# Two norms around a residual: the second sum of squares taken from three sums made beside the products, and products begun on several outputs at once

## The chip, the cores and the metric

One core of one Trainium2 chip. The metric is the time of one launch in microseconds (us). Weights and inputs lie in the chip's DRAM in float32. The names of the engines are those of the profile: PE is TensorE (matmuls), PEld its weight loads, DVE VectorE, ACT ScalarE, POOL GpSimd, SP the queue that issues nearly all weight loads.

## The reference, cut to what matters

The program is two blocks of a network, one behind the other, on 256 tokens ("latents") of width 1024, the second block with 256 context tokens beside them. The change lies in the second block, where each of two layers does this (`fn` is the mixer first, and a gated convolution FFN then):

```python
def rmsnorm(x, g):
    xf = x.astype(jnp.float32)
    y = xf * lax.rsqrt(jnp.mean(xf * xf, axis=-1, keepdims=True) + EPS)
    return (y * g.astype(jnp.float32)).astype(x.dtype)

hl = modulate(rmsnorm(xl, norm_g[layer, 0]), mod_l[0], mod_l[1])
...
xl = xl + mod_l[2] * rmsnorm(yl, norm_g[layer, 1])
hl = modulate(rmsnorm(xl, norm_g[layer, 2]), mod_l[3], mod_l[4])
xl = xl + mod_l[5] * rmsnorm(conv_ffn(hl, ...), norm_g[layer, 3])
```

So between two big products stand two norms in a row: the output y of the one is normed and added to the residual x, and the new x is normed again, scaled and shifted, to be the input h of the next. With r the inverse root of y's mean square and Y = gate·g·y, the new x is X + r·Y, and its sum of squares is sum(X·X) + 2r·sum(X·Y) + r²·sum(Y·Y). Layer 0 does this for context and latents (512 columns), layer 1's mixer for both and the rest for the latents alone (256 columns).

## The kernel before, in words

Activations lie transposed in SBUF: 8 tiles (KD = 8) of 128 features each by 512 columns of tokens, 256 of context (CTX) and 256 of latents (LAT). `k.X` is the residual, `k.H` the input of a product, `Y` the gated output of one. Weights stream through a ring of 11 slots of 1 MB ("units" of 16 tiles of 128 by 128, RING = 11, UT = 16); SP refills a slot when the last matmul of its unit is done (`refill`). A product with 8 input tiles is `gemm` (L255): output after output, and within one the 8 input tiles. Its results go to PSUM banks 0 to 3 in turn. A matmul of the program is two records on PE in the trace.

Each stage is an `nc.Block()`: every engine has its own list there, and the next block starts when all have ended theirs. The change touches three crossings from one block to the next, called here:

- **A**, layer 0: from `stage_square` (the mixer's output product, 512 columns) to `stage_conv_ffn` (the FFN's up products, 512 columns);
- **B**, from layer 0's FFN (its down product) to `stage_rwkv_project`, layer 1's first products, whose input is shifted and mixed on DVE (XX, XB) tile by tile, and whose first 8 outputs are for the 256 latents;
- **C**, layer 1: from `stage_square` to `stage_conv_ffn`, 256 columns each.

At each the class `AfterY` (L629) does the work. While the product before runs, `Beside` has ACT square each output (L579) and POOL add up outputs 0 to 6 (L586). Behind the last output, in the next block: PE sums those squares over features with matmuls against a column of ones (`add_up`, L508, one for each 128 columns), DVE, ACT and DVE take mean, root and inverse (L516, L523, L518), PE spreads the inverse over all partitions of bank 5 (`to_all`, L528), and DVE scales Y by it (`part`, L654). DVE adds the even tiles of Y to X (L657), POOL the odd ones (L664). ACT squares each tile of the new X (L673) into one of two buffers, PE adds it up (L508, 32 matmuls at 512 columns), ACT waits for PE to give a buffer back. Then mean, root, inverse and spread once more, and DVE scales X into H (L613), ACT scales and shifts H for each half (L621), and the product waits for its input tiles one by one (L272, `ready`). At B the DVE makes, behind all of that, -h (L3026), two shifted additions (L3016) and the mixed input (L3020) of each tile.

The modulation of the next layer is itself a product, of 24 units, run beside layer 0's FFN (`Modulation.unit`, L306: four matmuls of 32 rows by 512 columns); `weave` sets where its units stand among the FFN's in the order of weights, in pairs after every few units. `Finish` copies, turns and takes its result during the FFN's last outputs.

The edit also touches `Plan`, `woven` (the order of the weights in DRAM) and `block2_even` and its like for layer 1, where the objects are made.

## Time and profile before

| | |
|---|---|
| median of 3 runs | 3330.53 us (3325.06 to 3331.04) |
| the profiled execution | 3328.68 us, span 3326.8 us, mean granted clock of TensorE 0.952 |
| PE busy | 3102.2 us, 93% of the span |
| DVE busy | 1033.2 us, 31% |
| ACT busy | 587.9 us, 18% |
| POOL busy | 230.6 us, 7% |
| DMA | 577.07 MB, 173 GB/s over the span |

In the rows further down, a row of the timeline gives start and duration in us, engine, line, operation, output<-input, the count of instructions merged, and in brackets how long the engine sat idle before and what ended that. A row of the windows gives the window, and for each engine the busy us and (x) instructions, then the granted clock of TensorE (1.00 is 2.4 GHz, 0.50 is 1.2 GHz) and the share and rate of DMA. Matmul ends are modelled.

### The profile page before, as it was taken

Reading aid. Unit: us, or ns where it says so; the run is one execution under the profiler, and the core shown is the slowest. Engines: PE = TensorE matmul, PEld = TensorE weight load, DVE = VectorE, ACT = ScalarE, POOL = GpSimd, SP = SyncE. Lnnn points to the kernel's source line nnn. Section 1 sums busy time; section 2 is a strip of 40 time slices with the busy share of each in tenths; the row PEclk is TensorE's granted clock in tenths of the full one; section 3 lists DMA queues with packets and bytes.
Section 4 is the critical chain, followed back from the end, with each engine's and each line's share of the span. In section 5 each row is a group of like instructions: output and inputs, shape, how many; then the busy total and the mean of one; then the engine's idle time right before and its main releaser. Section 6 shows DMA issues by size and latency. Waiting matters only on the chain. (4 is left out here: it accounts for less than half of the span.)

```text
span 3326.8 us, 54854 instructions
## 1 busy us (share of the span) xinstructions
PE 3102.2 (93%) x24374; PEld 1905.5 (57%) x24374; DVE 1033.2 (31%) x2267; ACT 587.9 (18%) x1333; POOL 230.6 (7%) x205
## 2 busy tenths in 40 slices
PE   7999998999999999899888999999897888888998
PEld 5899884533333333446664444444645687777887
DVE  4365105211101110240451433400404555651650
ACT  1011113200000000220342100000203434432100
POOL 0000000000000000000221000000001231220000
PEclk8999999899999999899898999999798999897999
DMA  9755549499988899520003133333111000004340
GB/s 378 301 187 218 181 171 421 165 383 391 390 347 361 359 386 398 240 76 26 3 1 139 76 127 139 127 126 126 57 38 48 25 15 14 14 3 191 128 151 13
DMA packets 88494, 577.07 MB, mean 173 GB/s; under 512 B 9536, under 2 KB 15936, under 8 KB 20672
## 3 DMA queue, kind: packets, MB, share of 16 engines
q1 hardware_dynamic: 84800, 568.27, 43.8%
q10 hardware_dynamic: 3456, 5.24, 0.4%
q8 instruction: 195, 3.19, 0.4%
q14 instruction: 43, 0.35, 0.0%
HBM read 567.19 MB, written 6.29 MB: 172 GB/s over the span
## 5 line engine op out<-in xcount | busy, mean ns | idle before, releaser
L272 PE MATMUL ps<-H,ring 128*128 128x256 f32 (+1 forms) x2480 | 805.0, 487 | 12.3 <-ACT H L621 7.0
L272 PEld LDWEIGHTS ps<-H,ring 128*128 128x128 f32 x2480 | 478.2, 194 | 335.5 <-issue 298.1
L272 PE MATMUL ps<-W,ring 128*128 128x256 f32 (+1 forms) x1616 | 497.1, 469 | 13.4 <-DVE W L3020 8.0
L1865 PE MATMUL ps<-ring,W 128*32 128x512 f32 (+1 forms) x2816 | 461.4, 594 | 1.7 <-ACT H L1924 1.7
L272 PEld LDWEIGHTS ps<-W,ring 128*128 128x128 f32 x1616 | 309.3, 193 | 200.8 <-issue 170.5
L1865 PEld LDWEIGHTS ps<-ring,W 128*32 128x32 f32 (+1 forms) x2816 | 142.5, 123 | 306.7 <-issue 304.1
L1888 PE MATMUL ps<-ring,W 128*64 128x512 f32 (+1 forms) x1408 | 231.1, 594 | 0.0
L2146 DVE SCALAR_TENSOR_TENSOR W<-ps,vec,W 128x189 f32<-128x189 f32 (+3 forms) x396 | 173.3, 438 | 14.0
L3545 POOL TENSOR_TENSOR ring<-ring 128x512 f32<-128x512 f32 x96 | 124.5, 1313 | 526.2 <-DVE ring L3569 458.8
L1888 PEld LDWEIGHTS ps<-ring,W 128*64 128x64 f32 (+1 forms) x1408 | 70.9, 123 | 156.9 <-issue 156.9
L306 PE MATMUL ps<-ring,spread 128*32 128x512 f32 x768 | 101.1, 634 | 23.3 <-DMA ring<-weights 18.8
L1973 DVE TENSOR_TENSOR H<-ps,H 128x256 f32<-128x256 f32 x66 | 28.0, 425 | 303.5 <-ACT H L1915 303.5
L1915 ACT ACTIVATE H<-ps 128x256 f32<-128x256 f32 x66 | 25.3, 383 | 459.8 <-PE ps L1865 459.8
L2132 DVE TENSOR_SCALAR W<-ps,vec 128x512 f32<-128x512 f32 (+1 forms) x44 | 29.8, 677 | 235.1 <-PE ps L272 235.1
L3421 PE MATMUL ps<-ring 64*64 64x64 f32 x2560 | 89.9, 220 | 13.7 <-DVE ring L3659 13.6
L2168 ACT ACTIVATE W<-W 128x512 f32<-128x512 f32 (+1 forms) x44 | 23.0, 523 | 440.8 <-DVE W L2146 440.8
L3421 PEld LDWEIGHTS ps<-ring 64*64 64x64 f32 x2560 | 82.3, 134 | 18.8 <-issue 18.7
L3654 DVE TENSOR_TENSOR W<-W,ps 128x512 f32<-128x512 f32 x80 | 53.8, 672 | 120.2 <-PE ps L3436 120.2
L1020 PE MATMUL ps<-W 128*128 128x128 f32 x744 | 88.3, 275 | 0.0
L1020 PEld LDWEIGHTS ps<-W 128*128 128x128 f32 x744 | 85.5, 192 | 0.0
L3436 PE MATMUL ps<-W,ring 64*64 64x64 f32 x2560 | 83.7, 218 | 0.4 <-issue 0.4
L3436 PEld LDWEIGHTS ps<-W,ring 64*64 64x64 f32 x2560 | 79.7, 134 | 0.6 <-issue 0.5
(447 smaller groups left out, 3138.6 us busy)
## 6 DMA issues: line engine op xcount, KB each, us to landing
ring<-weights SPq DMA_DIRECT2D x528, 1024.0 KB, 7.9
rkv<-W ACTq DMA_DIRECT2D x16, 256.0 KB, 2.0
ring<-rkv SPq DMA_DIRECT2D x8, 512.0 KB, 3.6
X<-tokens SPq DMA_DIRECT2D x2, 1024.0 KB, 8.9
ring<-rw_tiles SPq DMA_DIRECT2D x8, 256.0 KB, 2.6
rkv<-W ACTq DMA_DIRECT2D x8, 128.0 KB, 2.3
ring<-rkv SPq DMA_DIRECT2D x8, 128.0 KB, 3.7
out<-X SPq DMA_DIRECT2D x8, 128.0 KB, 1.9
```

Of the source, the lines that this page charges most:

```text
L272: mm = pe.matmul(out(o), lhsT=k.ring[:, k.slot(at), p * P:(p + 1) * P], rhs=rhs(kk), start=kk == 0 and not (shared_bank and o % 2), stop=k ...
L306: mm = pe.matmul(k.ps[32 * q:32 * q + 32, self.bank, :], lhsT=self.spread[:, 4 * half + q, start:start + 32], rhs=k.ring[:, k.slot(place), ...
L1020: mm = pe.matmul(self.bank(bank), lhsT=a[:, kk * P:(kk + 1) * P], rhs=b[:, kk, :], start=start and kk == 0, stop=stop and kk == 3, skip_gr ...
L1865: mm = pe.matmul(ps[at:at + n, r, :], lhsT=moe.Hg[:, kt, FIRST * e + first:FIRST * e + first + n], rhs=w[e][:, kk * WIDE:(kk + 1) * WIDE], ...
L1888: mm = pe.matmul(ps[to:to + n, 3 - 3 * half + r, :], lhsT=moe.A[:, f, r, to:to + n], rhs=w[e][:, at:at + 512], start=f == 0, stop=f == KF - 1,
L1973: dve.tensor_tensor(moe.G[:, r, :], ps[:, r, S:2 * S], moe.G[:, r, :], ALU.mult).then_inc(sem["g"].sem, 1)
L2132: link(dve.tensor_scalar(y, x, w(1, 1), k.v("fcb", layer * KF + f), ALU.mult, ALU.add))
L2146: ins = dve.scalar_tensor_tensor(yo, xo, ww, yo, ALU.mult, ALU.add)
L3421: mm = pe.matmul(ps[half(e), bank, CH * n:CH * n + CH], lhsT=sc.OT[z][l % 2][half(e), n, :], rhs=sc.M[z][half(e), n, :], start=True, stop= ...
L3436: mm = pe.matmul(ps[half(e), bank, CH * n:CH * n + CH], lhsT=sc.T1[z][half(e), n, :], rhs=sc.MT[j % 2][z][half(e), n, :], start=True, stop ...
L3545: pool.tensor_tensor(sc.OT[z][l % 2], lt, sc.level[z][l].unsqueeze(1).to_broadcast([P, 8, CH]), ALU.mult).then_inc(sem["ot"], 1)
L3654: add = dve.tensor_tensor(flat(MT), flat(MT), ps[:, (4 + 4 * (l - 1) + z) % 3, :], ALU.add)
```

## The change

1. `Ahead` takes the place of `Beside` at A, B and C. While the product before runs, DVE multiplies each output Y with X and with itself and adds these up over outputs 0 to 6 (`cross`). PE sums the three running totals (squares, X·Y, Y·Y) right behind its last matmul, still in the old block (`add_totals`), and in the new block only what belongs to the last output (`add_last`). The kept sum of X·X (`sums_of_x`) is brought up to date on DVE from the three sums, with four small operations, and its root and inverse are spread to bank 7. The 8 squares of the new X on ACT and their sums on PE are gone.
2. `AfterY.vector` works tile by tile: part, change, scale (tiles 0 and 1), then in pairs, with POOL adding tiles 3, 5 and 7.
3. The FFN's up products begin with outputs 0 and 1 abreast, input tile by input tile; in layer 0 the first 8 modulation units stand among them, one ahead of each input tile (`early`).
4. In `stage_rwkv_project` the first 8 outputs run abreast, two to a PSUM bank of 512 columns, for each input tile as it comes. DVE shifts and mixes a tile right behind scaling the next one (`then`), and -h is made by ACT. The copies out of PSUM start when both outputs of a bank are done; the next outputs wait for the copies of theirs.

```diff
-def weave(units, more):
+def weave(units, more, early=0):
-    order, v = [], 0
+    order, v = [(1, i) for i in range(early)], early
...
+class Ahead(Beside):
+    SUMS = 7
...
+    def cross(self, dve, link, o, Y):
+        y = Y[:, o, 0:self.n]
+        at = 2 if o == 0 else o % 2
+        for t, x in ((self.xy, self.k.X[:, o, self.cols]), (self.yy, y)):
+            ins = dve.tensor_tensor(t[at], x, y, ALU.mult)
...
+        if 1 <= o < KD - 1:
+            link.wait()
+            for t in (self.xy, self.yy):
+                ins = dve.tensor_tensor(t[2], t[2], t[at], ALU.add)
...
+    def add_totals(self, pe):
+        pe.wait_ge(self.added.sem, self.added.at(KD - 2))
+        self.add_up(pe, self.total, self.blocks)
+        pe.wait_ge(self.crossed.sem, self.crossed.at(2))
+        self.cross_up(pe, self.xy[2], 0)
+        self.cross_up(pe, self.yy[2], NB)
+
+    def add_last(self, pe):
+        pe.wait_ge(self.squares.sem, self.squares.at(KD))
+        self.add_up(pe, self.sq[1], self.blocks).then_inc(self.sums.sem, 1)
+        pe.wait_ge(self.crossed.sem, self.crossed.at(3))
+        self.cross_up(pe, self.xy[1], 0)
+        pe.wait_ge(self.crossed.sem, self.crossed.at(4))
+        self.cross_up(pe, self.yy[1], NB).then_inc(self.cross_sums.sem, 1)
...
 class AfterY(Norm):
+    PARTS, BY_POOL, OWN = (0, 1, 3, 2, 5, 4, 7, 6), (3, 5, 7), (0, 1, 2, 4, 6)
...
     def tensor(self, pe):
-        self.before.add_tiles(pe)
+        self.before.add_last(pe)
         self.before.to_all(pe)
-        for i in range(KD):
-            pe.wait_ge(self.rms.squares.sem, self.rms.squares.at(i + 1))
-            mm = self.rms.add_up(pe, self.sq[i % 2], self.rms.blocks)
-            mm.then_inc(self.rms.sums.sem if i == KD - 1 else self.summed.sem, 1)
         self.rms.to_all(pe)
...
+    def vector(self, dve, then=lambda i: None, later=0):
...
+        before.cross(dve, link, KD - 1, Y)
+        dve.wait_ge(before.sums.sem, before.sums.at(1))
...
+        dve.wait_ge(before.cross_sums.sem, before.cross_sums.at(1))
...
+        link(dve.tensor_tensor(tail, both[:, 1, own], r, ALU.mult))
+        link(dve.scalar_tensor_tensor(tail, both[:, 0, own], 2.0, tail, ALU.mult, ALU.add))
+        link(dve.tensor_tensor(tail, tail, r, ALU.mult))
+        link(dve.tensor_tensor(x, x, tail, ALU.add))
+        dve.tensor_scalar(rms.r[:, own], x, 1.0 / D, EPS, ALU.mult, ALU.add).then_inc(rms.mean.sem, 1)
...
+        for i in (0, 1):
+            part(i)
+            change(i)
+            if i == 0:
+                dve.wait_ge(rms.spread.sem, rms.spread.at(1))
+            scaled(i)
+        for i in (2, 4, 6):
+            part(i + 1)
+            part(i)
+            change(i)
+            scaled(i)
+            scaled(i + 1)
...
@@ stage_square @@
             gemm(k, pe, 8, KD, lambda kk: k.H[:, kk, cols], lambda o: k.ps[:, o % 4, 0:n], before, signals)
+            rms.add_totals(pe)
...
+            for o in range(KD - 1):
+                dve.wait_ge(k.act.sem, k.act.at(o + 1))
+                rms.cross(dve, link, o, Y)
...
@@ stage_conv_ffn @@
-    p = Plan(owner, ada.units)
+    p = Plan(owner, ada.units, early=min(KD, ada.units))
...
-                 plan=p, ada=ada, ready=pre.ready)
+                 plan=p, ada=ada, ready=pre.ready, abreast=2,
+                 more=(lambda kk: ada.unit(pe, p.place[1, kk], kk)) if ada.units else None)
...
+            for o in range(KD - 1 if ahead else 0):
+                dve.wait_ge(k.act.sem, k.act.at(KF + o + 1))
+                rms.cross(dve, link, o, Y)
...
@@ stage_rwkv_project @@
+    place = lambda o: k.ps[:, o // 2, (o % 2) * S:(o % 2) * S + S]
...
-                    if first_o + o >= 4:
-                        pe.wait_ge(k.act.sem, k.act.at(first_o + o - 3))
+                        pe.wait_ge(k.act.sem, k.act.at(2 * o + 2 if n == 1 and o < 4 else first_o + o - 3))
+                if n == 0:
+                    gemm(k, pe, KD, KD, lambda kk: XB[0][:, kk, LAT], place, before, signals, abreast=KD, shared_bank=True,
+                         ready=lambda eng, kk: eng.wait_ge(k.dve.sem, k.dve.at(kk + 1)))
+                    continue
...
+            def then(j):
+                if j >= 1:
+                    shift(j - 1)
+                    dve.wait_ge(shifted.sem, shifted.at(2 * j))
+                    mixed(0, j - 1)
+
+            pre.vector(dve, then, later=1)
```

The last FFN (layer 1) still ends with `Beside`, and `stage_last` is as before.

PE at crossing A, from the last product of `stage_square` into the FFN, before (a branch ends a block; L508 are the sums against ones, L528 the spreads):

```order
L272 MATMUL ps<-H,ring 128x512 x64
L2043 UNCONDITIONAL_BRANCH
L2101 UNCONDITIONAL_BRANCH
L508 MATMUL ps<-const,W 128x1 x8
L528 MATMUL ps<-const,sm 128x128 x4
L508 MATMUL ps<-const,W 128x1 x32
L528 MATMUL ps<-const,sm 128x128 x4
L272 MATMUL ps<-H,ring 128x512 x48
L306 MATMUL ps<-ring,spread 32x512 x8
```

and in the changed kernel (L632 are the sums of X·Y and Y·Y):

```order
L272 MATMUL ps<-H,ring 128x512 x64
L508 MATMUL ps<-const,W 128x1 x4
L632 MATMUL ps<-const,W 128x1 x8
L2140 UNCONDITIONAL_BRANCH
L2204 UNCONDITIONAL_BRANCH
L508 MATMUL ps<-const,W 128x1 x4
L632 MATMUL ps<-const,W 128x1 x8
L528 MATMUL ps<-const,sm 128x128 x8
L306 MATMUL ps<-ring,spread 32x512 x4
L272 MATMUL ps<-H,ring 128x512 x2
L306 MATMUL ps<-ring,spread 32x512 x4
L272 MATMUL ps<-H,ring 128x512 x2
```

Twelve sums stand ahead of the end of the block and twelve behind it, the 32 are gone, and a modulation unit (4 of L306) stands ahead of each pair of product matmuls.

DVE at crossing B, before, from the second mean to the first mixed tile (L613 scales X, L3026 is -h, L3016 the shifted additions, L3020 the mixing):

```order
L516 TENSOR_SCALAR sm<-ps 128x4
L518 RECIPROCAL sm<-sm 128x4
L613 TENSOR_TENSOR H<-X,ps 128x512 x8
L3026 TENSOR_SCALAR W<-H 128x512 x2
L3016 TENSOR_TENSOR W<-W,H 128x255
L3016 TENSOR_TENSOR W<-W,H 128x4x63
L3026 TENSOR_SCALAR W<-H 128x512
L3016 TENSOR_TENSOR W<-W,H 128x255
L3016 TENSOR_TENSOR W<-W,H 128x4x63
L3020 SCALAR_TENSOR_TENSOR W<-W,vec,H 128x256
```

and now (L726 part, L730 change, L737 scale, L3129 shifted additions, L3133 mixing):

```order
L726 TENSOR_TENSOR W<-W,ps 128x512
L730 TENSOR_TENSOR X<-X,W 128x512
L737 TENSOR_TENSOR H<-X,ps 128x512
L726 TENSOR_TENSOR W<-W,ps 128x512
L730 TENSOR_TENSOR X<-X,W 128x512
L737 TENSOR_TENSOR H<-X,ps 128x512
L3129 TENSOR_TENSOR W<-W,H 128x255
L3129 TENSOR_TENSOR W<-W,H 128x4x63
L3133 SCALAR_TENSOR_TENSOR W<-W,vec,H 128x256
L726 TENSOR_TENSOR W<-W,ps 128x512 x2
L730 TENSOR_TENSOR X<-X,W 128x512
L737 TENSOR_TENSOR H<-X,ps 128x512
```

The first mixed tile stands behind 6 full-width operations of DVE and its own 3, where 8 scalings, with the parts and changes of all tiles ahead of them, stood before it.

## Rows read from the trace of the kernel before

**Rows 1.** The page: busy time, share of the span, instructions.

```profile
PE 3102.2 (93%) x24374; PEld 1905.5 (57%) x24374; DVE 1033.2 (31%) x2267; ACT 587.9 (18%) x1333; POOL 230.6 (7%) x205
```

**Rows 2.** Timeline of crossing A, from the last product to the first.

```profile
1789.63 22.05 PE L272 MATMUL ps<-H,ring 128*128 128x512 f32 x51
...
1812.22 0.83 ACT L780 ACTIVATE W<-ps,sm 128x256 f32<-128x256 f32 x2
...
1813.35 2.14 PE L508 MATMUL ps<-const,W 128*128 128x1 f32 x16 [1.67 <-PEq L2043]
1815.54 0.16 DVE L516 TENSOR_SCALAR sm<-ps 128x4 f32<-128x4 f32 x1 [58.85 <-PE ps L508]
...
1816.20 2.07 PE L528 MATMUL ps<-const,sm 128*128 128x128 f32 x8 [0.70 <-DVE sm L518]
1818.31 1.28 DVE L654 TENSOR_TENSOR W<-W,ps 128x512 f32<-128x512 f32 x2 [2.17 <-PE ps L528]
1819.51 0.69 DVE L657 TENSOR_TENSOR X<-X,W 128x512 f32<-128x512 f32 x1
1819.67 7.04 POOL L664 TENSOR_TENSOR X<-X,W 128x512 f32<-128x512 f32 x4 [12.88 <-DVE W L654]
...
1820.92 13.81 PE L508 MATMUL ps<-const,W 128*128 128x1 f32 x64 [2.64 <-ACT W L673]
...
1837.54 4.87 DVE L613 TENSOR_TENSOR H<-X,ps 128x512 f32<-128x512 f32 x8 [2.16 <-PE ps L528]
1838.27 7.97 ACT L621 ACTIVATE H<-H,mod 128x256 f32<-128x256 f32 x16 [3.10 <-DVE H L613]
```

**Rows 3.** Timeline of PE alone behind crossing A.

```profile
1839.51 44.47 PE L272 MATMUL ps<-H,ring 128*128 128x512 f32 x96 [2.00 <-ACT H L621]
1883.91 1.92 PE L306 MATMUL ps<-ring,spread 128*32 128x512 f32 x16
```

**Rows 4.** Windows at crossing A: the clock is the figure before the DMA share.

```profile
1814.00:1817.00 3.00, 2.30 (x16) 2.21 (x15) 0.34 (x2) 0.20 (x1) 0.00 (x0) 0.65 0.62 259
...
1845.00:1848.00 3.00, 3.00 (x7) 1.24 (x7) 0.00 (x0) 2.52 (x4) 0.00 (x0) 0.90 0.00 0
```

**Rows 5.** Timeline of crossing B and of ACT's copy of the eighth output.

```profile
2303.48 19.13 PE L272 MATMUL ps<-W,ring 128*128 128x512 f32 x44
...
2353.70 0.74 DVE L3016 TENSOR_TENSOR W<-W,H 128x255 f32<-128x255 f32 x2
...
2355.37 0.48 DVE L3020 SCALAR_TENSOR_TENSOR W<-W,vec,H 128x256 f32<-128x256 f32 x1
...
2355.99 2.53 PE L272 MATMUL ps<-W,ring 128*128 128x256 f32 x4 [7.79 <-DVE W L3020]
...
2391.07 0.38 ACT L3050 ACTIVATE W<-ps 128x256 f32<-128x256 f32 x1 [3.07 <-PE ps L272]
```

**Rows 6.** A window at crossing B, where the clock rises.

```profile
2365.00:2369.00 4.00, 4.00 (x13) 3.24 (x13) 4.00 (x7) 0.38 (x1) 0.00 (x0) 0.64 0.10 33
```

**Rows 7.** Timeline of crossing C, and a window where the clock rises.

```profile
3049.65 15.70 PE L272 MATMUL ps<-H,ring 128*128 128x256 f32 x72
...
3078.68 1.22 PE L528 MATMUL ps<-const,sm 128*128 128x128 f32 x4 [0.69 <-DVE sm L518]
3079.94 2.74 DVE L613 TENSOR_TENSOR H<-X,ps 128x256 f32<-128x256 f32 x8 [1.31 <-PE ps L528]
...
3081.14 17.08 PE L272 MATMUL ps<-H,ring 128*128 128x256 f32 x70 [1.24 <-ACT H L621]
...
3084.00:3086.00 2.00, 2.00 (x10) 1.68 (x9) 0.00 (x0) 1.71 (x2) 0.00 (x0) 0.84 0.00 0
```

**Rows 8.** Four outputs abreast in layer 0's first product: timeline and window.

```profile
1396.58 30.33 PE L272 MATMUL ps<-H,ring 128*128 128x512 f32 x64 [1.27 <-ACT H L746]
...
1401.00:1404.00 3.00, 3.00 (x7) 1.30 (x6) 2.81 (x10) 2.32 (x5) 0.00 (x0) 0.85 0.00 0
```

**Rows 9.** Weight loads early in layer 0's FFN: count, KB, median us to landing.

```profile
ring<-weights SPq DMA_DIRECT2D x6, 1024.0 KB, 4.8
```

More of the change, by code:

```diff
@@ L198, with __init__ @@
 class Plan:
-    def __init__(self, owner, more=0, seven=0):
+    def __init__(self, owner, more=0, seven=0, early=0):
         self.product = {}
         self.units = -(-len(owner) // UT)
-        self.order = weave(self.units, more)
+        self.order = weave(self.units, more, early)
         self.place = {x: i for i, x in enumerate(self.order)}
@@ L629, with __init__ @@
 class AfterY(Norm):
-    def __init__(self, k, cols, scale, shift, before, sq, Y):
-        super().__init__(k, cols, scale, shift, Rms(k, "after", range(cols.start // P, cols.stop // P), 404))
+    PARTS, BY_POOL, OWN = (0, 1, 3, 2, 5, 4, 7, 6), (3, 5, 7), (0, 1, 2, 4, 6)
+    def __init__(self, k, cols, scale, shift, before, Y):
+        super().__init__(k, cols, scale, shift, Rms(k, "after", range(cols.start // P, cols.stop // P), 404, squares=0))
+        self.rms.SPREAD = 7
         self.before, self.Y, self.n = before, Y, cols.stop - cols.start
-        self.sq = [x[:, 0:self.n] for x in sq]
-        self.part, self.changed, self.summed = k.shared("part", KD), k.shared("changed", KD // 2), k.shared("summed", KD - 1)
-        self.odd = k.shared("odd_changed", KD // 2)
+        self.part, self.changed, self.odd = k.shared("part", KD), k.shared("changed", KD - 3), k.shared("odd_changed", 3)
+        self.sums_of_x, self.tail = k.sm[:, 408:412], k.sm[:, 412:416]
@@ L660, in pool, with scalar @@
     def pool(self, pool):
         k, cols = self.k, self.cols
-        for i in range(1, KD, 2):
-            pool.wait_ge(self.part.sem, self.part.at(i + 1))
+        for i in self.BY_POOL:
+            pool.wait_ge(self.part.sem, self.part.at(self.PARTS.index(i) + 1))
             pool.tensor_tensor(k.X[:, i, cols], k.X[:, i, cols], self.Y[:, i, 0:self.n], ALU.add).then_inc(self.odd.sem, 1)
-    def scalar(self, act):
+    def scalar(self, act, then=lambda i: None):
+        k = self.k
         self.before.take_root(act)
+        self.rms.take_root(act)
@@ L668, in scalar @@
         for i in range(KD):
-            done = self.odd if i % 2 else self.changed
-            act.wait_ge(done.sem, done.at(i // 2 + 1))
-            if i >= 2:
-                act.wait_ge(self.summed.sem, self.summed.at(i - 1))
-            act.activation(self.sq[i % 2], self.k.X[:, i, self.cols], ACT.Square).then_inc(self.rms.squares.sem, 1)
-        super().scalar(act)
+            act.wait_ge(self.normed.sem, self.normed.at(i + 1))
+            for h, c in self.halves:
+                ins = act.activation(k.H[:, i, c], k.H[:, i, c], ACT.Identity, scale=self.scale(i, h), bias=self.shift(i, h))
@@ L678 @@
+            ins.then_inc(self.h.sem, 1)
+            then(i)
 class AfterFirst(Norm):
@@ L2071, in stage_square, with stage_conv_ffn @@
     k.unit += U_SQ
-def stage_conv_ffn(k, layer, cols, Y, ada, pre, rms, finish=None):
+def stage_conv_ffn(k, layer, cols, Y, ada, pre, rms, finish=None, ahead=True):
     nc = k.nc
@@ L2119, in _ @@
                  signals, first=down0 * KD, plan=p, ada=ada)
+            if ahead:
+                rms.add_totals(pe)
         @block.vector
@@ L3043, in _, with then @@
         def _(act):
-            pre.scalar(act)
+            def then(i):
+                pre.ready(act, i)
+                act.activation(XX[:, i, :], k.H[:, i, :], ACT.Copy, scale=-1.0).then_inc(turned.sem, 1)
+            pre.scalar(act, then)
             for o in range(24):
-                act.wait_ge(k.mm.sem, k.mm.at(out_done[o]))
+                act.wait_ge(k.mm.sem, k.mm.at(out_done[o | 1 if o < KD else o]))
                 if o >= 4:
@@ L3049, in _ @@
                 c = tokens(o // 8)
-                act.activation(out[:, o % 4, c], k.ps[:, o % 4, c], ACT.Copy).then_inc(k.act.sem, 1)
+                act.activation(out[:, o % 4, c], place(o) if o < KD else k.ps[:, o % 4, c], ACT.Copy).then_inc(k.act.sem, 1)
                 act.wait_ge(k.act.sem, k.act.at(o + 1))
@@ L3738, in wide_units, with woven @@
     return w.reshape(2, 4, P, n // WIDE, WIDE).transpose(3, 0, 2, 1, 4).reshape(-1, P, 4 * WIDE)
-def woven(own, *more):
+def woven(own, *more, early=0):
     more = np.concatenate(more)
-    return np.stack([more[u] if kind else own[u] for kind, u in weave(len(own), len(more))])
+    return np.stack([more[u] if kind else own[u] for kind, u in weave(len(own), len(more), early)])
 def cols(v):
```

96 lines of the change are left out of this document (66 added, 30 removed).

## The prediction, made blind

> **What bounds the kernel now.** I read the page first: PE is busy 93% of the span, the other engines a third or less [rows 1]. So time can come only out of stretches in which PE has nothing useful to do or does it at half clock. The change touches three crossings (A, B, C), and the timeline of each shows such a stretch. At A the last product ends at 1811.68 (1789.63 + 22.05) and the next starts at 1839.51 [rows 2, 3]: 27.8 us. At B it is 2322.61 to 2355.99, 33.4 us [rows 5], and at C 3065.35 to 3081.14, 15.8 us [rows 7]. PE is not idle all that time: at A 64 records of sums take 13.81 us [rows 2], which is the second sum of squares. The windows give the clock: at A the mean of 0.65 over 1814 to 1817 means that it fell at about 1814.9, 3.2 us behind the last product and in spite of the sums that ran, and 0.90 over 1845 to 1848 that it rose at about 1845.6, 6.1 us behind the first product [rows 4]. At B it rose at 2367.9, 11.9 us behind the first, thinly spaced products [rows 6], at C at 3084.6, 3.5 us behind [rows 7].
>
> Behind each crossing PE runs without a gap (96 records in 44.47 us at A, 70 in 17.08 at C [rows 3, 7]), so I take it that what a crossing gives goes to the end of the program. The sum is made against the profiled execution, 3328.7 us; the median of the runs is 1.8 above it. A measurement of this kernel tells some 0.2%, 6.7 us, from no change.
>
> **Prices.** A product record of 512 columns takes 22.05 / 51 = 0.432 us [rows 2], one of 256 columns 15.70 / 72 = 0.218 [rows 7]. A sum record takes 2.14 / 16 = 0.134 with the clock mostly full and 13.81 / 64 = 0.216 at half. A spread takes 2.07 [rows 2], at C 1.22 [rows 7]. A block ends 0.30 us behind its last engine (ACT ends at 1813.05, PE starts at 1813.35), and three small steps on DVE, ACT, DVE take 1816.20 - 1815.54 = 0.66, 0.22 each [rows 2].
>
> **Crossing A.** The sums of the totals are 12 matmuls, 24 records, right behind the last product: 3.2 us, to 1814.9; they replace ACT's tail to 1813.05 as what ends the block, and 0.3 more gives 1815.2. `add_last` is 24 records. All at half clock, as the clock falls just there: 5.2, to 1820.4 (3.2 if it fell later; that is the bound below). DVE's two multiplications of the last output (0.69 each, by the addition L657 [rows 2]) and its mean and inverse lie beside that. Then the two spreads, 4.1, to 1824.5: the second needs the new chain on DVE, four small operations and the three steps, 0.88 + 0.66 = 1.5 us behind the last sum, less than the first spread takes. Part and change of tile 0 (1.4) also fit beside the second spread. From scaling to product took 1839.51 - 1837.54 = 1.97 [rows 2, 3]: the first product would start at 1826.5, 13.0 earlier. But a modulation unit (1.92 / 2 = 0.96 us [rows 3], twice that at half clock) now stands ahead of it, needs nothing of the norm and fills those 2 us. So PE's useful work begins at 1824.5 where it began at 1839.5: **15.0 us**. The loss to half clock behind it was 44.47 - 96 x 0.432 = 3.0 us and I keep it.
>
> Do the tiles come fast enough? DVE makes 8 parts, 5 changes and 8 scalings at 0.6 to 0.69, 1.9 us a tile; PE wants 4 records and a unit a tile, 2.7 at full clock. POOL's addition takes 7.04 / 4 = 1.76 beside DVE [rows 2], and DVE comes back to it behind a part, a change and a scaling, 1.9: just in time. So PE never waits behind tile 0. The early units also want weights sooner: the first refill is asked for at the first unit and lands in 4.8 us [rows 9], and 11 slots are full at the start, where a unit of products lasts 13.8 us. I cost that at nothing; if the loads took 13.8 each, each would show whole.
>
> **Crossing B.** Same steps: 2322.61 + 3.2 + 0.3 + 5.2 + 4.1 = 2335.4. Then DVE scales tile 0, makes part, change and scaling of tile 1 (2.7), two shifted additions (0.74), the mix (0.48) and two short waits: 4.1, to 2339.5, 16.5 earlier than 2355.99 [rows 5]. The eight outputs took from there to 2391.07, 35.1 us; their 128 records want 27.9, and the rest was half clock and DVE's pace. Abreast, each tile is 3.5 us of work on arrival, so PE has no gap and I charge only 3.0 for the clock, as at A: 30.9, to 2370.4. **20.7 us.** DVE's pace is 5.9 us for two tiles (five operations of 0.69 at most, two times 1.27), the last tile is mixed at 2358.3, and PE needs it at 2366.9. The copies out of PSUM, now bunched, stand behind each other at 0.38 and an issue: ACT has bank 0 free about when PE wants it. The -h on ACT (0.6 a tile) lies beside DVE.
>
> **Crossing C.** 12 records of totals 1.6, 0.3, 12 of `add_last` 2.6: 3069.85. Here the DVE chain (1.5) is longer than the spread (1.22): 3071.35, spread to 3072.6, scaling to product 3081.14 - 3079.94 = 1.2 [rows 7]: 3073.8, 7.3 earlier. The clock took 1.8 before (17.08 - 70 x 0.218); it may take 3.0 now. I take **6.7 us**. DVE's pace is 0.98 a tile against 0.87 for two outputs abreast, but PE starts at half clock and behind.
>
> **The products beside** pay nothing: DVE's four operations for an output, under 2.8 us, fit into the 6.9 us of one at A (3.5 and 1.7 at C), where DVE is idle. Behind output 6 come ACT's tail (1811.68 to 1813.05 at A) and these four, so its totals are ready 6.9 - 1.4 - 2.8 = 2.7 us before PE asks, at C about 3.5 - 0.8 - 1.7 = 1.0.
>
> Sum: 15.0 + 20.7 + 6.7 = 42.4. From 3328.7 that is 3286.3, from the median 3288.1; I say 3287.
>
> **A rule against it.** The program already runs four outputs abreast, in four banks in turn: 64 records in 30.33 us, and 0.85 over 1401 to 1404 puts the rise of the clock at 1401.9, 5.3 us behind the start [rows 8]. So cycling banks did not keep the clock low there, with 512 columns and no other matmuls between. The Trainium skill, "TensorE: Matmul & The Clock Gate", section "A second HAM failure mode: psum-queue depth-cycling", says that a product which cycles through PSUM banks leaves PE idle for short moments and the clock swings between its levels. By that rule the abreast parts would lose most of what they give; the row speaks against it, but no row has units of 32 rows between, nor eight outputs of 256 columns two to a bank.
>
> **The rivals.**
> - *The clock stays low longer.* At B it took 11.9 us to rise behind thin work [rows 6]. If that is the measure everywhere, each crossing loses 6.0 instead of 3.0, 3.0 and 2.4: 9.6 us, 3297. For it: sums and 32-row units may count for little, as the sums did at 1814.9. Against it: A and rows 8, both dense, 5.3 and 6.1. Chance 0.12.
> - *DVE becomes the bound at B.* If waits between its steps make a tile 4.5 us, the last is mixed at 2371.0 and the outputs end at 2374.5, 4.1 later: 3291. It decides from 4.1 us a tile on. Against it: the pace above comes from rows with the same waits. Chance 0.06.
> - *Slower: the clock does not rise at all while outputs run abreast.* The place is the first tiles behind each crossing. Their work is 8 x (1.73 + 0.96) = 21.5 at A, 27.9 at B, 7.0 at C, in all 56.4 us at full clock; at half it costs 56.4 more, then 3.0 on each plain run behind, less the 8.4 already in the sum: 57.0 against 42.4. That is 14.6 slower than the median before, 3345. It decides once more than about three quarters of that work runs at half. Against it [rows 8]. Chance 0.03.
> - *The change doesn't do what it says*: the totals wait in PE's queue for DVE, or the small chain takes the place of the squares. Even then the squares of X are gone, with 13.8 us of sums at A [rows 2] and as much at B; some 2 us at each crossing come back, 3293. Chance 0.04.
>
> **How the numbers follow.** The forecast has the remaining 0.75. Its own bounds: `add_last` at full clock gives 4 us more, a rise of the clock after 3.5 us another 2.6, the lowest of the runs 5: 3275. Above, the low clock and a little of a DVE pace: 3299. So 3275 to 3299. Faster by more than 6.7 us in all cases but the slower one and oddities: 0.95; within 0.2%: 0.02; slower 0.03.
>
> **What would show it.** In the changed profile: 24 short records right behind the last product and 24 behind the branch; no squares of X on ACT; first product about 15 us (modulation unit), 16.5 and 7.3 us earlier relative to the last product; at B the eighth output's copy some 48 us behind the last product instead of 68; the clock at 1.00 within 6 us of the first dense work. Wrong would be: PE idle between tiles, a clock of 0.50 through the abreast part, or PE waiting for DMA behind the early units.

## The result, and the profile after

The changed kernel takes 3272.97 us (median of 4 runs, 3269.43 to 3274.41) against 3329.82 for the kernel before beside it. The ratio is 0.983, 95% interval 0.9813 to 0.9847: **56.9 us faster**. The forecast was 42.4 us, 3287, with a range down to 3275, so the sign was right, the forecast gain was too small, and the time fell below the range. The profiled execution took 3269.43 us, a span of 3267.5 against 3326.8, 59.3 less, at a mean granted clock of 0.962 against 0.952.

The page of the changed kernel, which answers to [rows 1]: PE has 80 records fewer and is busy 35 us less, while the span is 59 shorter; DVE has 62 us more work.

```profile
PE 3067.4 (94%) x24294; PEld 1876.8 (57%) x24294; DVE 1094.7 (34%) x2358; ACT 580.4 (18%) x1317; POOL 223.5 (7%) x202
```

**Where the time went.** I cut both traces at the same instructions, into stretches that add up to the span.

| stretch, us | before | after | less | forecast |
|---|---|---|---|---|
| start to the last product ahead of A | 1811.7 | 1812.8 | -1.2 | 0 |
| A, and on to the last product ahead of B | 510.9 | 493.7 | 17.2 | 15.0 |
| B, and on to the end of layer 1's first products | 195.5 | 171.2 | 24.3 | 20.7 |
| the scan, to the last product ahead of C | 547.3 | 538.5 | 8.8 | 0 |
| C, and on to the last down product | 171.7 | 163.5 | 8.2 | 6.7 |
| last down product and the end | 89.8 | 87.8 | 1.9 | 0 |

The three crossings gave 49.7 us where 42.4 were forecast; another 9.5 came from stretches that I had taken to stay as they are (how far these repeat is told with the first two runs below).

PE at A in the changed kernel (columns as in [rows 2, 3]):

```profile
1784.78 28.06 PE L272 MATMUL ps<-H,ring 128*128 128x512 f32 x65
1812.67 0.95 PE L508 MATMUL ps<-const,W 128*128 128x1 f32 x8
1813.48 1.93 PE L632 MATMUL ps<-const,W 128*128 128x1 f32 x16
1815.71 1.64 PE L508 MATMUL ps<-const,W 128*128 128x1 f32 x8 [0.30 <-PEq L2140]
1817.21 3.55 PE L632 MATMUL ps<-const,W 128*128 128x1 f32 x16
1820.62 3.78 PE L528 MATMUL ps<-const,sm 128*128 128x128 f32 x16
1824.33 1.94 PE L306 MATMUL ps<-ring,spread 128*32 128x512 f32 x8
1826.31 1.98 PE L272 MATMUL ps<-H,ring 128*128 128x512 f32 x4
...
1846.68 53.48 PE L272 MATMUL ps<-H,ring 128*128 128x512 f32 x124
```

The reader is to see that the old 64 records of sums are gone, that PE has no wait but the block's 0.30 us, and that the first unit comes 11.5 us behind the last product (1812.84), where the forecast had 12.8 and in the kernel before the first useful matmul came at 27.8. The windows of the same place show why the tiles then run fast:

```profile
1815.00:1818.00 3.00, 2.70 (x16) 2.65 (x16) 1.63 (x4) 0.20 (x1) 0.00 (x0) 0.65 0.71 300
1818.00:1821.00 3.00, 3.00 (x15) 3.00 (x16) 0.13 (x1) 0.00 (x0) 0.00 (x0) 0.50 0.03 5
...
1824.00:1827.00 3.00, 2.96 (x12) 0.76 (x12) 2.62 (x5) 1.09 (x2) 0.00 (x0) 0.64 0.00 0
1827.00:1830.00 3.00, 3.00 (x14) 0.87 (x13) 2.93 (x5) 1.09 (x2) 1.27 (x1) 1.00 0.83 289
```

The clock falls at about 1815.9, in spite of sums that run back to back, and rises at 1826.2 (0.64 over 1824 to 1827), 1.8 us behind the first unit. Before it rose 6.1 us behind the first product [rows 4].

B, PE's timeline:

```profile
2289.65 16.90 PE L272 MATMUL ps<-W,ring 128*128 128x512 f32 x39
2306.39 0.95 PE L508 MATMUL ps<-const,hat 128*128 128x1 f32 x8
...
2310.31 3.06 PE L632 MATMUL ps<-const,H 128*128 128x1 f32 x16
2313.23 3.79 PE L528 MATMUL ps<-const,sm 128*128 128x128 f32 x16
2321.12 99.06 PE L272 MATMUL ps<-W,ring 128*128 128x256 f32 x290 [4.11 <-DVE W L3133]
```

Against [rows 5] the first product starts 14.6 us behind the last one (2306.55) instead of 33.4, and then PE has no gap for 99 us: DVE's eight tiles never hold it up. The windows:

```profile
2308.00:2311.00 3.00, 2.70 (x25) 2.65 (x24) 1.37 (x3) 1.46 (x2) 0.00 (x0) 0.98 0.80 328
2314.00:2317.00 3.00, 3.00 (x15) 2.72 (x13) 1.92 (x6) 0.21 (x1) 0.00 (x0) 0.50 0.00 0
2317.00:2320.00 3.00, 0.01 (x1) 0.00 (x0) 2.88 (x5) 1.90 (x4) 0.00 (x0) 0.89 0.01 3
2320.00:2323.00 3.00, 1.88 (x5) 1.56 (x6) 2.93 (x6) 1.54 (x3) 1.26 (x1) 0.68 0.00 0
2323.00:2326.00 3.00, 3.00 (x12) 2.55 (x11) 2.89 (x6) 1.72 (x4) 0.00 (x0) 0.75 0.00 0
2326.00:2329.00 3.00, 3.00 (x16) 2.64 (x15) 2.93 (x6) 1.72 (x3) 1.04 (x1) 1.00 0.00 0
```

The clock rises right behind the two spreads, while PE stands idle (0.89 with 0.01 us busy), falls again at about 2321.1 (0.68), and is up for good at about 2324.5, 3.4 us behind the first product; in [rows 6] it took 11.9.

ACT's copies of the eight outputs, of which the fifth and the eighth are shown:

```profile
2354.13 0.38 ACT L3165 ACTIVATE W<-ps 128x256 f32<-128x256 f32 x1 [3.26 <-DMA rkv<-W]
...
2360.27 0.38 ACT L3165 ACTIVATE W<-ps 128x256 f32<-128x256 f32 x1 [0.46 <-ACT W L3165]
```

The fifth, sixth and seventh wait for DMAs that empty their buffers (3.26 us at the fifth), and the eighth follows right behind them. It comes 53.7 us behind the last product (68.5 before), not the 48 that I gave as a sign; PE is not held up by it.

C, timeline and windows:

```profile
2994.64 21.53 PE L272 MATMUL ps<-H,ring 128*128 128x256 f32 x99
...
3017.70 0.58 PE L508 MATMUL ps<-const,W 128*128 128x1 f32 x4 [0.30 <-PEq L2140]
...
3019.10 0.69 PE L528 MATMUL ps<-const,sm 128*128 128x128 f32 x4
3020.78 1.21 PE L528 MATMUL ps<-const,sm 128*128 128x128 f32 x4 [1.00 <-DVE sm L722]
3023.23 27.13 PE L272 MATMUL ps<-H,ring 128*128 128x256 f32 x114 [1.24 <-ACT H L769]
```

```profile
3018.00:3020.00 2.00, 1.79 (x15) 1.59 (x14) 1.25 (x8) 0.20 (x1) 0.00 (x0) 1.00 0.93 393
3020.00:3022.00 2.00, 1.21 (x4) 0.91 (x4) 1.17 (x5) 0.20 (x1) 0.00 (x0) 0.71 0.18 74
3026.00:3028.00 2.00, 2.00 (x7) 1.61 (x6) 1.93 (x5) 0.89 (x3) 0.72 (x1) 0.58 0.00 0
```

All sums and the first spread are over before the clock falls: 1.00 up to 3020. The second spread waits 1.00 us for DVE's chain, as forecast, and the first product comes 7.1 us behind the last one (3016.17) instead of 15.8 [rows 7].

### The profile page after: what moved, and what is told of

It is laid out like the page before. It is cut to its first block and busy times, and to the rows that moved or that the text cites. A ratio compares the mean times of both kernels' runs of the same rounds, so it can differ in the third digit from the quotient of the medians.

```text
span 3267.5 us, 54770 instructions
## 1 busy us (share of the span) xinstructions
PE 3067.4 (94%) x24294; PEld 1876.8 (57%) x24294; DVE 1094.7 (34%) x2358; ACT 580.4 (18%) x1317; POOL 223.5 (7%) x202
## 5 line engine op out<-in xcount | busy, mean ns | idle before, releaser
L272 PE MATMUL ps<-H,ring 128*128 128x256 f32 (+1 forms) x2480 | 802.1, 486 | 10.3 <-ACT H L678 3.7
L272 PE MATMUL ps<-W,ring 128*128 128x256 f32 (+1 forms) x1616 | 490.5, 465 | 9.1 <-DVE W L3133 4.1
L306 PE MATMUL ps<-ring,spread 128*32 128x512 f32 x768 | 104.9, 652 | 20.6 <-DMA ring<-weights 16.2
```

What stands on the lines that cost most here:

```text
L272: mm = pe.matmul(out(o), lhsT=k.ring[:, k.slot(at), p * P:(p + 1) * P], rhs=rhs(kk), start=kk == 0 and not (shared_bank and o % 2), stop=k ...
L306: mm = pe.matmul(k.ps[32 * q:32 * q + 32, self.bank, :], lhsT=self.spread[:, 4 * half + q, start:start + 32], rhs=k.ring[:, k.slot(place), ...
```

## The experiments

Times are medians; the kernel before ran beside each. "The scan" is the recurrent scan of layer 1 with what follows it up to the last product ahead of C, without its lead-in of some 7 us. "Tile to product" is the part of it from the start of its last tile to that product.

**Both kernels again**, unedited, to see which stretches repeat.

> The kernel before, unchanged. In the profile of before, the recurrent scan of layer 1 and what follows it up to the last product ahead of crossing C took 540.1 us, in that of the changed kernel 530.8, though no line of it changed; with the last down product it makes some 11 us that the prediction does not have. Theory 1 (fixed by the program: what PE issues ahead of the scan decides how its clock and a stall of 3.2 us without a releaser fall): a second profile shows 540 again within 1 us, the stall at the same place. Theory 2 (chance of each execution): it lies anywhere between 530 and 540, and the stall may be gone. Time 3325 to 3331 by both.

> The changed kernel, unchanged. Theory 1: the scan to the last product ahead of C takes 530.8 us again within 1 us. Theory 2: anywhere between 530 and 540. Time 3269 to 3275 by both.

Before again: 3327.09 against 3328.06, ratio 0.9999 (0.9989 to 1.0008). After again: 3273.88, 0.9838 (0.9822 to 0.9855). The crossings repeat: A was 510.92 and 493.71 us, B 195.49 and 171.16, C 171.63 and 163.43, each within 0.1 us of the first traces. The scan does not: 537.1 us without its lead-in, against 540.1 in the first trace of the same kernel, and 533.8 against 530.8. So in this second pair the spans differ by 51.8 us, of which the crossings have 49.7 and the untouched stretches 2.1, not 9.5; the medians differ by 54.2.

**None of the three abreast**, all else of the change kept.

```diff
-    p = Plan(owner, ada.units, early=min(KD, ada.units))
+    p = Plan(owner, ada.units, early=0)
...
-                 plan=p, ada=ada, ready=pre.ready, abreast=2,
-                 more=(lambda kk: ada.unit(pe, p.place[1, kk], kk)) if ada.units else None)
+                 plan=p, ada=ada, ready=pre.ready)
...
-                    gemm(..., signals, abreast=KD, shared_bank=True,
+                    gemm(..., signals, abreast=1, shared_bank=True,
```

> The new norms and the order of DVE's work stay, but every product runs output after output, and the modulation units stand where they stood. Theory of the prediction: PE then waits at A, B and C for each tile in turn. At B the first output ends no sooner than the last tile, 19 us behind the first one, with 3.4 us of work in it: about 17 us of the gain at B are lost. At A the first output takes 15 us for 6.9 of work, so 8 are lost, and the unit ahead of the first tile 1 more. At C the first output ends with the last tile 7.5 us behind the first, 3.5 of work: 3 lost. Together 29: some 3300 us. Rival (the clock, not the work abreast, gave the gain): PE's gaps between tiles keep the clock at half and more is lost, over 35, or, if the tiles come faster than PE takes them, under 10.

3305.01 us, ratio 0.9934 (0.9917 to 0.995). A takes 501.4, B 190.3, C 167.9: the abreast parts are worth 7.7 us at A, 19.1 at B and 4.4 at C, 31.2 in all. The new norms alone gave the rest: 9.5, 5.2 and 3.8 at the crossings, 18.5 in all, or 23 in the medians, which hold the untouched stretches too. The traces show what abreast does. B of this kernel, timeline and windows:

```profile
2331.02 1.19 PE L272 MATMUL ps<-W,ring 128*128 128x256 f32 x2 [4.10 <-DVE W L3132]
2335.32 1.22 PE L272 MATMUL ps<-W,ring 128*128 128x256 f32 x2 [3.11 <-DVE W L3132]
```

```profile
2330.00:2336.00 6.00, 1.87 (x4) 1.00 (x4) 5.82 (x12) 3.26 (x7) 1.27 (x1) 0.50 0.00 0
...
2342.00:2348.00 6.00, 2.26 (x5) 0.82 (x5) 5.82 (x12) 3.20 (x7) 1.27 (x1) 0.50 0.00 0
```

Two records a tile leave PE idle and the clock at 0.50 for twenty us. Abreast, 16 records a tile do both at once: they fill the waits, and they bring the clock up.

**Abreast alone**, at A and C, on the old norms.

```diff
-    p = Plan(owner, ada.units)
+    p = Plan(owner, ada.units, early=min(KD, ada.units))
...
-                 plan=p, ada=ada, ready=pre.ready)
+                 plan=p, ada=ada, ready=pre.ready, abreast=2,
+                 more=(lambda kk: ada.unit(pe, p.place[1, kk], kk)) if ada.units else None)
```

> The kernel before with two outputs abreast in the FFNs and the 8 modulation units early; old norms. Theory: at A the unit fills 1 us of the 2 ahead of the first product, and nothing else is gained, since PE at half clock was slower than the tiles came; the interleaving costs 0.2 us a tile. At C nothing. So no change within 2 us, 3328. Rival (the abreast work is worth something of its own): 5 us or more faster.

3326.40, ratio 0.9999 (0.999 to 1.0009). In its trace A takes 508.1, 2.8 less than before, and C 171.6, nothing less. So the abreast parts and the new norms are not a sum of two gains: where the old norm makes all tiles ready nearly at once, there is little to fill. The eight outputs abreast at B, the largest part, were not tried on the old norms; they could have won at most some 7 us there, by an estimate, since the eight outputs took 35.1 us for 27.9 of work.

**No early units** at A, two outputs abreast kept.

```diff
-    p = Plan(owner, ada.units, early=min(KD, ada.units))
+    p = Plan(owner, ada.units, early=0)
...
-                 plan=p, ada=ada, ready=pre.ready, abreast=2,
-                 more=(lambda kk: ada.unit(pe, p.place[1, kk], kk)) if ada.units else None)
+                 plan=p, ada=ada, ready=pre.ready, abreast=2)
```

> The changed kernel with two outputs abreast in layer 0's FFN but no modulation units among its first tiles: they stand where they stood before. B and C stay. Theory: at A the first product starts at the same time, 13.5 us behind the last one, but the unit no longer fills the 2 us ahead of it, and with only two records a tile more to do PE waits for tiles once the clock is up: the last tile comes some 13 us behind the first, two outputs are 13.8 us of work; 2 to 3 us slower than the changed kernel. Rival (the units cost by interleaving, 0.2 us a tile, more than they fill): as fast or 1 us faster.

3272.38, ratio 0.9837 (0.9822 to 0.9853): no slower than the change. A itself takes 496.2, 2.4 us more than after, which this ratio (0.15%, 5 us, to either side) cannot show. Timeline and windows of A:

```profile
1824.64 25.95 PE L272 MATMUL ps<-H,ring 128*128 128x512 f32 x54 [2.00 <-ACT H L769]
```

```profile
1824.00:1827.00 3.00, 2.36 (x3) 1.17 (x4) 2.92 (x5) 1.59 (x4) 0.90 (x1) 0.50 0.00 0
1827.00:1830.00 3.00, 3.00 (x7) 1.09 (x6) 2.97 (x5) 1.33 (x3) 0.45 (x2) 0.86 0.00 0
```

What the early units are worth, by filling the 2 us ahead of the first product, is thus 2.4 us, seen in the trace alone: the 2.00 us wait is back, and the clock is up at about 1827.8, 16.7 us behind this kernel's last product (1811.1), where it took 13.3 with the units.

**The clock held up at B and C** with matmuls on constants, 16 (5 at C), behind the second spread.

```diff
+        for i in range(self.warm):
+            pe.matmul(self.k.ps[:, Rms.COLUMNS, 0:P], lhsT=self.k.ident, rhs=self.k.ident, start=True, stop=True)
...
-    return AfterY(k, both, *parts2(k, 1, 0), rms, Y)
+    return AfterY(k, both, *parts2(k, 1, 0), rms, Y, warm=16)
```

> The changed kernel with 16 matmuls of 128 columns more behind the second spread at B and 5 at C, where PE idles 4.1 and 1.2 us ahead of the first product; their output is used by nobody. Theory (dense matmuls of 128 columns raise the clock as products do; two spreads back to back raised it at B and PE's idle time let it fall again): at B the clock stays at 1.00 through the first tiles and the eight outputs end 1.7 us sooner, at C the first two outputs end 1 to 2 us sooner; 2 to 4 us faster than the changed kernel. Rival (the sums and spreads don't count): no change, or slower by the tail of the added matmuls, 1 us.

3274.09, ratio 0.9838 (0.9825 to 0.9851), no gain. B of this kernel:

```profile
2325.76 4.58 PE L272 MATMUL ps<-W,ring 128*128 128x256 f32 x20 [0.62 <-DVE W L3136]
```

```profile
2319.00:2322.00 3.00, 2.85 (x24) 2.64 (x23) 2.93 (x7) 2.56 (x5) 0.02 (x1) 1.00 0.01 3
```

The clock is at 1.00 from the first product on, but PE then catches up with DVE and waits 0.62 us; the stretch from the first product on is 155.8 instead of 156.6, 0.8 less. At C the first product comes 1.5 us later. So what half clock still costs behind B is under a us, because DVE's next tile is the other limit there.

**The scan.** Its code is not touched, yet every one of the four profiles with the old norms (before, again, abreast alone, two loads below) has 537 to 540 us there and every one of the four with the new ones (after, again, none abreast, no early) 531 to 534; the means are 539.1 and 531.8, 7.3 apart. Most of it lies behind the start of the last tile: tile to product is 122.7 to 124.1 in the old ones and 116.6 to 117.0 in the new. The list of waits of the kernel before has there

```profile
PE ps L3279 <- issue: 3.2, 1, 3.2
```

a wait for which this list knows no releaser, at 3020, while SP's eleven weight loads run. Windows of before, and of after at about the same distance from the start of the last tile (2942.5 and 2899.1):

```profile
3020.00:3024.00 4.00, 0.77 (x16) 0.75 (x14) 0.24 (x1) 0.00 (x0) 0.00 (x0) 0.90 1.01 418
3024.00:3028.00 4.00, 3.30 (x53) 2.71 (x49) 0.05 (x1) 0.66 (x2) 0.00 (x0) 0.50 1.02 424
...
3036.00:3040.00 4.00, 4.00 (x10) 3.12 (x10) 0.00 (x0) 0.00 (x0) 0.00 (x0) 0.50 0.00 0
```

```profile
2972.00:2976.00 4.00, 3.98 (x122) 3.70 (x121) 0.58 (x2) 0.48 (x2) 0.00 (x0) 0.87 1.01 422
...
2980.00:2984.00 4.00, 2.33 (x10) 1.53 (x11) 0.77 (x3) 0.62 (x2) 0.00 (x0) 0.50 1.01 420
...
2988.00:2992.00 4.00, 4.00 (x15) 3.35 (x14) 0.00 (x0) 0.00 (x0) 0.00 (x0) 0.74 0.08 31
```

Before, PE stalls and then runs some 17 us at 0.50, up to 3040; after, it has no such stall, and some 10 us at 0.50. Two things could move the stall: when the loads run (the theory of the burst), and where the instructions stand in PE's stream, since the change takes 80 records away ahead of it. Eight kernels went to that.

Two loads in flight at most, in the kernel before:

```diff
             for u in range(RING):
+                if u >= 2:
+                    sp.wait_ge(k.w_in[k.slot(u - 2)], k.landed(u - 2))
```

> The kernel before; the 11 weight loads that SP issues at once at the end of the scan are held to two in flight. Six profiles so far: from the start of the scan's last tile to the last product ahead of C it took 122.9, 124.1 and 122.7 us with the old norms, 117.0, 116.8 and 116.9 with the new ones, and with the old ones PE stood for 3.2, 1.8 and 1.8 us late in the scan, with no releaser, while the loads ran at some 420 GB/s. Theory (PE's own instructions are late behind the burst of loads, and the stall then drops the clock): with two loads in flight the stall falls below 1 us and that stretch takes 117 to 119; the program is 4 to 6 us faster, 3323. Rival (the difference is the clock's alone): 123 again, no change.

3328.38 against 3328.16, ratio 0.9996 (0.9985 to 1.0006). The stall is 2.0 us, tile to product 122.7: nothing moved. With two in flight the loads still ran at 361 GB/s over 3010 to 3020, where the kernel before had 428, so most of the burst stayed and this tells nothing apart.

One load at a time, in either kernel:

```diff
             for u in range(RING):
+                if u >= 1:
+                    sp.wait_ge(k.w_in[k.slot(u - 1)], k.landed(u - 1))
```

> The kernel before with the 11 weight loads at the end of the scan held to one in flight (e5 held them to two, and they ran at the same rate). Each is then asked for only when the last has landed, so the DMA engines rest between. Theory (PE's instruction load waits behind weight packets): the stall of 1.8 to 3.2 us goes below 1 us, the stretch takes 117 to 120, the program 3 to 6 us less. Rival (the wait is the load's own latency, whatever else the DMA does): 123 and a stall of 2 us.

> The same for the changed kernel, which has hardly a stall there. Both theories: the stretch takes 117 as before and the time is that of the changed kernel within 2 us, 3273, unless a product waits for its weights: the fourth unit is needed some 50 us behind the first load, when ten have come.

3348.04 (1.0063, 1.0043 to 1.0083) and 3297.75 (0.9911, 0.9892 to 0.9931), 18 us slower than the kernel before beside it, and some 24 slower than the changed kernel in its other runs. In the kernel before no stall over 0.2 us is left at this place, and the last tile's matmuls end 4 us sooner, but the next block starts only when SP has issued its last load, and SP now takes 50 us, to 3054.3; the first product behind starts at 3054.8:

```profile
3004.18 50.16 SPq L3195 DMA_DIRECT2D ring<-weights  x11
```

The same gentle loads without that: four in the scan, one at a time, and seven in the block behind.

```diff
+            for u in range(4, RING) if preload else ():
+                sp.dma_start(k.ring[:, k.slot(u), :], k.a["weights"][k.unit + u]).then_inc(k.w_in[k.slot(u)], 16)
...
-            for u in range(RING):
+            for u in range(4):
+                if u >= 1:
+                    sp.wait_ge(k.w_in[k.slot(u - 1)], k.landed(u - 1))
```

> The kernel before; at the end of the scan SP issues only 4 weight loads, one at a time, and the other 7 at the start of the next block. From the scan's last tile to its last 256-column matmul it took 85.3 to 86.8 us in four profiles of the old norms, 81.5 with one load in flight. Theory (the burst of weight loads holds up PE's instruction loads): 81 to 82.5, the block ends as before, the program 3 to 5 us faster, 3325. Rival (the place of the instructions alone): 85 to 87, no change, or slower by waits for the later loads.

> The same for the changed kernel, where that stretch took 79.8 to 81.6 us and 77.9 with one load in flight. Theory: 78, some 2 to 3 us faster than the changed kernel, 3271. Rival: 80 to 81, 3273.

The kernel before becomes 3325.45 against 3329.85, ratio 0.9988 (0.9979 to 0.9997); the one after stays at 3273.38, 0.9834 (0.982 to 0.9848). Tile to product is 117.5 in the old kernel so paced and 117.0 in the new. The waits and windows of the first:

```profile
PE ps L3283 <- issue: 0.5, 1, 0.5
```

```profile
3021.00:3025.00 4.00, 3.51 (x110) 3.11 (x106) 0.58 (x2) 0.48 (x2) 0.00 (x0) 1.00 0.63 246
3025.00:3029.00 4.00, 2.36 (x27) 1.39 (x26) 0.42 (x1) 0.88 (x3) 0.00 (x0) 0.68 0.02 6
...
3033.00:3037.00 4.00, 3.30 (x9) 2.72 (x10) 0.55 (x2) 0.00 (x0) 0.00 (x0) 0.54 0.53 174
```

With loads at 246 GB/s instead of 424 the stall is down to 0.5 us, the half clock to some 10 us as in the changed kernel, and the old kernel's last tile is nearly as quick as the new one's. Its whole scan, 537.1 us, is only 2.0 below the mean of its kind, though, as the part ahead of the last tile was longer. The changed kernel had no such stall to lose (0 and 0.6 us in its two traces), so it gains nothing.

Matmuls added between B and the scan, 32 in either kernel and 16 in the changed one, move the stream and leave the loads alone:

```diff
+            for i in range(32):
+                pe.matmul(k.ps[:, 4, 8:9], lhsT=k.ident, rhs=k.ones[:, 0:1], start=True, stop=True)
```

> The changed kernel with 32 short matmuls more behind the products of layer 1's first stage, as many as the two norms ahead of it have fewer: PE has then as many instructions ahead of the scan as before. They cost 32 x 2 x 0.13 = 8.3 us where they stand. Theory (what differs in the scan is where PE's instruction loads fall against the burst of weight loads, set by the count of instructions ahead): the stretch from the scan's last tile to the last product takes 122 to 124 again, with a stall of 1 to 3 us, and the program is 14 slower than the changed kernel. Rival: 117 as in the changed kernel, 8 slower.

> The kernel before with the 32 short matmuls of e6, at the same place; they cost some 8 to 10 us there. PE's instructions come in loads of 16 KB, so what may count is where in a load PE stands when the burst of weight loads begins. By the order of the two programs 32 matmuls more put the kernel before where the changed kernel stands, one load further. Theory (place in the load): the stretch from the scan's last tile to the last product takes 117 us as in the changed kernel, not 122.7 to 124.1, and no stall without a releaser over 1 us; the program is 2 to 4 slower than before, 3331. Rival (it is not the place): 123 again, 8 to 10 slower, 3337.

> The changed kernel with 16 short matmuls more, half of e6's; they cost 4 to 5 us. e6 gave 119.3 for the stretch and 537.8 for the whole scan, e7, with 21 of another kind, 119.7 and 534.5, the changed kernel 117.0 and 116.8, 530.8 and 533.8. Theory (place in the load): between those, 117 to 120, the whole 532 to 537. Rival (chance): below 117 or above 120, or the whole over 538.

| | median, us | ratio (95%) | pads' own | scan | tile to product | stalls over 0.2 in the last tile |
|---|---|---|---|---|---|---|
| before with 32 | 3332.63 | 1.0012 (1.0002 to 1.0021) | 10.3 | 534.7 | 118.4 | none |
| after with 32 | 3286.35 | 0.9872 (0.9857 to 0.9887) | 9.9 | 537.8 | 119.3 | 1.2 |
| after with 16 | 3275.83 | 0.9842 (0.9823 to 0.9861) | 3.5 | 534.1 | 119.0 | 2.3 |

Matmuls that do nothing made the old kernel's scan 4.5 us shorter than the mean of its kind and the new one's 6.0 longer, 2.5 of it in the last tile; in the last tile neither came out as forecast (117 for the old, 118.4 measured; 122 to 124 for the new, 119.3). For the old kernel both count: with its instructions moved no stall over 0.2 us is left in the last tile, with its loads paced one of 0.5. The stall is not the whole of it: the kernel without early units has one of 1.5 us and the shortest last tile of all, 116.6.

**What PE waits for in a stall.** The trace also holds the DMA packets that bring instructions, 195 of them for 3.19 MB on the page of the kernel before, 16 KB each. One starts at 3020.78, 0.8 us into the stall of 3.2 us, and the stall ends 2.5 us behind its start. The DMA view of 3020.7 to 3021.95 has it beside 75 packets of weights; that of 3020.02 to 3020.75 has none:

```profile
q8 instruction: 1, 0.02, 5.5%
```

In the scans of the sixteen profiles PE has 43 waits of over 0.3 us without a releaser, and every one ends 2.2 to 3.0 us behind the start of such a packet; a moment picked at random lies so in one case of seven or eight. So the stalls are PE waiting for its next instructions. The eight of 1 us and over all lie beside the burst of weights; the others reach 0.96. In the four old kernels that stall, the packet comes 365 to 468 PE records behind the one before it, weight loads and waits counted; with paced loads the same packet comes after 270, and PE waits 0.5 us. In the changed kernel it is as late (388 records, at 2979.53), but there PE needs 10 matmuls in the next 4 us, and nothing waits. That is how the place in the stream and the loads work together.

## Why the prediction was right in its mechanism and short in its size

**A: forecast 15.0, measured 17.2.** The steps went as written: totals behind the last product, 24 records behind the branch, no second round of sums, the unit first. The term mis-sized is the clock. "The loss to half clock behind it was 3.0 us and I keep it": the rise came 1.8 us behind the start of the first useful record, where I had 6.1, so 0.9 us are lost and not 3.0. The sums were also a little shorter, 11.5 us to the first unit and not 12.8: the totals took 2.6 us and not 3.2, and the two spreads 3.7 and not 4.1; the clock fell 3.1 us behind the last product, as before. Against that stands a cost that I did not have: a tile's four product and eight unit records take 2.91 us (1829.22 to 1832.13), not 2.69, 1.8 us over eight tiles. The refill of the ring, costed at nothing, cost nothing.

**B: forecast 20.7, measured 24.3.** The first product came at 14.6 and not 16.9 us, because `add_last` still ran at full clock up to about 2310.9 (3.9 us, not 5.2; 0.98 over 2308 to 2311) and the totals took 2.6, not 3.2. The eight outputs took 29.5 us and not 30.9, the clock again. "All at half clock, as the clock falls just there" had a bound beside it; the bound was nearer.

**C: forecast 6.7, measured 8.2.** The first product came 7.1 us behind the last, not 8.45, as the clock had not fallen yet; the half clock behind it, up to 3027.7, cost 0.6 of that again.

**The products beside cost nothing**, as said: the last product ahead of A ends at 1811.1 to 1814.4 in the profiles with them and at 1811.3 to 1813.9 in those without.

**The step that failed** is the second paragraph's "what a crossing gives goes to the end of the program", read as: all else stays. It rested on rows of 44.47 us behind A and 17.08 behind C, and put every stretch beyond them at nothing. None of the crossings' gain was given back, but the untouched stretches moved by 9.5 us. The crossings' own 49.7 us would have meant 3281 from the median before, within the range; the rest took the time below it. That rest is in part chance: it was 9.5 us in the first pair of traces and 2.1 in the second. The terms of the crossings that were mis-sized, above all the clock, are the other part of the miss, 7.3 us. Of the scan's share some 5 us are shown to hang on a late instruction load and a spell of half clock that move with PE's stream and with the loads. The last down product's 1.9 us go the same way. Its first 3 us, in a window of the kernel before and then of the one after:

```profile
3237.00:3240.00 3.00, 2.95 (x10) 2.49 (x11) 0.00 (x0) 0.00 (x0) 0.00 (x0) 0.71 0.72 306
```

```profile
3180.00:3183.00 3.00, 3.00 (x15) 2.64 (x14) 0.00 (x0) 0.00 (x0) 0.00 (x0) 1.00 0.63 262
```

Both had a wait of 2.0 us for DVE in front. In the one the clock fell behind it, in the other it did not. No run here shows why; the paced old kernel and the one with 32 pads have 88.1 there, the new one with paced loads and the one with none abreast 89.5, so it is not the norms either.

**The rivals.** That the clock stays low longer went the other way at each place. DVE as the bound at B is refuted by 99 us of PE without a gap; its tiles came at 3.1 us each in pairs. The rule of the Trainium skill ("TensorE: Matmul & The Clock Gate", section "A second HAM failure mode: psum-queue depth-cycling") tells of a bfloat16 kernel in which PE idles for moments between its groups of matmuls. It is not borne out for this form, where PE had no gap: eight outputs in four banks, two to a bank, ran at 1.00 from 2326 on, and so did two outputs with units between from 1827 on. "None abreast" is the direct test, 31 us slower. The change did what it says.

**What stays open.** Why the clock held through the wait of 2 us ahead of the last down product in some kernels and not in others; what moves the scan ahead of its last tile, 413 to 420 us in these profiles; and what holds the instruction packet back beside the weight loads. That it comes later is shown; that it queues behind their packets is argued. No version that was tried is measurably faster than the change; those without early units, with the clock held, and with paced loads are level with it.

## What to carry to other kernels

When a norm must stand between two products, take its sums from quantities that exist before the last output is done, and give the next product several outputs to work on per input tile. The second is worth more than the first here (31.2 us against 18.5 at the crossings), but on top of it: alone, it gave 2.8 us at A and nothing at C, and at B it was not tried alone. When pricing the clock behind a restart, let the bound reach down to none lost, since how long it took to rise behind the old, thinner work was no measure; and leave some us of room on either side for untouched stretches whose PE stream or clock shifts. A wait of PE without a releaser can be looked up among the instruction packets of the DMA view.

## What the runs showed of the hardware

- TensorE's clock fell in the middle of sums against a column of ones that kept PE 100% busy (0.50 over 1818 to 1821), and rose right behind 16 records of 128 columns at B, when PE had already gone idle.
- PE's stalls without a releaser in the scan are waits for instructions: all 43 of over 0.3 us end 2.2 to 3.0 us behind the start of a 16 KB packet on the instruction queue. The largest, 3.2 us beside weight loads at some 420 GB/s, went when 32 matmuls were added 500 us ahead of it. A comparison of two kernels whose instruction counts differ can carry some 5 us of this, 0.15% here.
- When DVE and POOL add tiles of 512 columns at the same time, DVE's addition takes 1.27 us in the pairs and 0.69 alone (its multiplications 0.64 to 0.69), and POOL's takes 1.27 where it had taken 1.76 [rows 2].
